# Gate columns turned, one modulation unit per slot, and no barrier before the context's projection

## The reference

```
a = rms_norm(h, norm_mix_pre)
z = a @ w_in                                  # 2048 x 4656
u, g_lru, q, kc, vc, ksel, vsel, kw, vw, gts = split(z)
y_lru = rglru_mixer(u, g_lru, ...)            # conv of 4 taps, gates, scan over time, times gelu
y_nsa = nsa_mixer(q, kc, vc, ksel, vsel, kw, vw, gts, ...)
y = concat(rms_norm(y_lru), rms_norm(y_nsa))  # then @ w_out, post norm, residual
```

## Time and profile before

| | us |
|---|---|
| runs | 2850.11, 2856.14, 2848.38 (median 2850.11) |
| the profiled execution | 2852.62, its span 2850.8 |
| PE busy | 2786.9 (98%) |
| DVE busy | 1748.4 (61%) |
| ACT busy | 1310.5 (46%) |
| POOL busy | 310.1 (11%) |
| chain that ended last, share on PE | 89% |

### The profile page before, as it was taken

How to read it: one execution, slowest core, us unless ns; L and a number is a source line. 1 busy time by engine, 2 the same in 40 slices (tenths; PEclk the granted TensorE clock), 3 DMA queues, 4 the chain that set the end, 5 groups by cost and what they waited for, 6 DMA issues and landing times.

```text
span 2850.8 us, 33136 instructions
## 1 busy us (share of the span) xinstructions
PE 2786.9 (98%) x13404; PEld 2188.3 (77%) x13404; DVE 1748.4 (61%) x2325; ACT 1310.5 (46%) x1912; POOL 310.1 (11%) x258
## 2 busy tenths in 40 slices
PE   8999899999989999999999999999999999999998
PEld 5777788888867777777777887887778888877786
DVE  4654646665646565565544664658876665788764
ACT  5362335554534344434533444454555454455553
POOL 0000100000022000001001110124201011321001
PEclk9999899999999999999999999999999999999999
DMA  8776474455588776767777756575345556454543
GB/s 300 272 264 239 162 261 162 155 207 199 185 276 287 251 244 218 254 222 251 255 261 244 263 200 206 190 253 168 126 142 179 204 191 201 164 170 132 171 172 123
DMA packets 293015, 600.34 MB, mean 211 GB/s; under 512 B 12514, under 2 KB 19370, under 8 KB 290944
## 3 DMA queue, kind: packets, MB, share of 16 engines
q1 hardware_dynamic: 279824, 548.07, 56.8%
q0 software_dynamic: 10656, 46.94, 4.4%
q10 hardware_dynamic: 2384, 3.22, 0.3%
HBM read 585.02 MB, written 13.17 MB: 210 GB/s over the span
## 4 chain that ended last, share of the span: by engine, by line
PE 89%; DVE 6%; DMA 2%; ACT 1%; POOL 0%; issue 0%; SPq 0%; DVEq 0%; ACTq 0%; POOLq 0%
PE ps L684 25%; PE ps L686 25%; PE ps L685 25%; PE ps L696 3%; DVE wlo L1838 2%; DVE bvx L2369 2%; PE ps L874 1%; PE ps L1106 1%; PE ps L1124 1%; PE ps L663 1%; PE ps L859 1%; DMA raw<-in_w_in_dram 1%; DMA raw<-in_mlp_w_dram 1%; ACT whi L1293 1%; PE ps L926 1%; PE ps L826 0%
## 5 line engine op out<-in xcount | busy, mean ns | idle before, releaser
L1838 DVE TENSOR_TENSOR wlo<-raw,whi 128x1024 fp32r<-128x1024 f32 x840 | 1040.6, 1263 | 774.6 <-ACT whi L1293 770.3
L1293 ACT ACTIVATE whi<-raw 128x1024 fp32r<-128x1024 f32 x840 | 868.8, 1050 | 1215.7 <-PE ps L686 809.0
L684 PE MATMUL ps<-whi,ay_hi 128*128 128x512 f32 x1728 | 689.4, 399 | 4.7 <-DVE ay_lo L2335 2.4
L686 PE MATMUL ps<-whi,ay_lo 128*128 128x512 f32 x1728 | 674.7, 390 | 0.0
L685 PE MATMUL ps<-wlo,ay_hi 128*128 128x512 f32 x1728 | 674.3, 390 | 0.0
L684 PE MATMUL ps<-whi,ax_hi 128*128 128x512 f32 (+1 forms) x1632 | 653.6, 400 | 9.9 <-DVE wlo L1838 7.5
L686 PE MATMUL ps<-whi,ax_lo 128*128 128x512 f32 (+1 forms) x1632 | 637.1, 390 | 0.0
L685 PE MATMUL ps<-wlo,ax_hi 128*128 128x512 f32 (+1 forms) x1632 | 636.7, 390 | 0.0
L684 PEld LDWEIGHTS ps<-whi,ax_hi 128*128 128x128 f32 x1632 | 310.8, 190 | 115.8 <-issue 41.6
L684 PEld LDWEIGHTS ps<-whi,ay_hi 128*128 128x128 f32 x1728 | 325.5, 188 | 83.1 <-issue 12.1
L686 PEld LDWEIGHTS ps<-whi,ay_lo 128*128 128x128 f32 x1728 | 325.1, 188 | 69.3
(11 more groups left out here) (478 smaller groups left out, 1996.9 us busy)
## 6 DMA issues: line engine op xcount, KB each, us to landing
raw<-in_w_in_dram SPq DMA_DIRECT2D x208, 1024.0 KB, 5.1
raw<-in_mlp_w_dram SPq DMA_DIRECT2D x128, 1024.0 KB, 6.4
raw<-in_w_mod_dram SPq DMA_DIRECT2D x96, 1024.0 KB, 7.4
raw<-in_w_out_dram SPq DMA_DIRECT2D x64, 1024.0 KB, 5.1
raw<-in_ple_gate_dram SPq DMA_DIRECT2D x16, 1024.0 KB, 5.1
z2c<-zsc POOLq DMA_DIRECT2D x13, 512.0 KB, 3.1
G<-bias_d ACTq DMA_DIRECT2D x4, 768.0 KB, 6.3
h<-in_ctx_dram POOLq DMA_DIRECT2D x1, 2048.0 KB, 8.5
```

The costliest lines, as they stand in the source:

```text
L684: mm(dst, hi_[:, kk, tt], whi[:, x.s % 2, k, 0:w], start=(nth == 0), stop=False)
L686: ins = mm(dst, lo_[:, kk, tt], whi[:, x.s % 2, k, 0:w], start=False, stop=(nth == KT - 1))
L1293: A(whi[:, x.s % 2, 2 * kh:2 * kh + 2, 0:w], raw[:, x.slot, 2 * kh:2 * kh + 2, 0:w], ACT.Copy).then_inc(hi_ready, 1)
L1838: V.tensor_tensor(wlo[:, x.s % 2, ks, 0:w], raw[:, x.slot, ks, 0:w], f32v(whi[:, x.s % 2, ks, 0:w]), ALU.subtract).then_inc(lo_ready, 1)
```

## The change

- `MOD0_AT` puts one modulation unit behind each unit from 3 to 34: chunk m in slots 3+4m to 6+4m. The column sums move into the middle of the unit after a chunk's last slot.
- `in1g` is one unit: its 16 row tiles by 48 columns are loaded in one transfer, the 48 columns become the stationary operand and 256 rows of the activations move: 48 products into 48 partitions. DVE copies the result (`zgT`, in the place of `modp_a`), PE transposes it back beside the first context unit, DVE scales it.
- The LRU's last steps lie one or two slots earlier, `prep("m2_01")` stands in slots 34 to 36, with `tmp` in `qT`'s place. The barrier is gone; waits on single semaphores stand for it. The high and low parts of the LRU's result are made in `nsa()`, slots 1 and 2.
- The start: the rest of x is issued when its first quarter has landed, the further weights when the first ones have.
- POOL copies h to memory first, then loads `cu`, `ca`, `cb` and the weights together; the sigmoid's product comes after the first squares.

```
-MOD0_AT = [(3, 4, 5, 6), (8, 9, 10, 11), (13, 14, 15, 16), (18, 19, 20, 20), (22, 23, 24, 25), (27, 28, 29, 29),
-           (31, 32, 33, 34), (36, 37, 38, 38)]
+MOD0_AT = [tuple(range(3 + 4 * m, 7 + 4 * m)) for m in range(8)]
...
-        for n in range(40):
+        for n in range(37):
...
                 if n == 1:
+                    sp.wait_ge(ev("x_in0"), 48)
                     sp.dma_start(h[:, :, CH:2 * CH], x_rows[:, :, CH:2 * CH]).then_inc(ev("x_in1"), 16)
                     sp.dma_start(h[:, :, 2 * CH:D], x_rows[:, :, 2 * CH:D]).then_inc(ev("x_in2"), 16)
+                    sp.wait_ge(raw_in[0], 16)
...
+                    if i == 2 and middle is not None:
+                        middle()
...
+            def gates_unit(x, A):
+
+                pe.wait_ge(lo_ready, 2 * x.s + 2)
+                pe.wait_ge(half_out, x.a - 1)
+                hi_, lo_ = A
+                w = GATES
+                dst = ps[0:w, half(x, 0)[1], 0:SEQ]
+                wh, wl = used(whi[:, x.s % 2], x), used(wlo[:, x.s % 2], x)
+                for k in range(KT):
+                    c_ = slice(k * w, k * w + w)
+                    one = mm(dst, wh[:, c_], hi_[:, k, :], start=(k == 0), stop=False)
+                    mm(dst, wh[:, c_], lo_[:, k, :], start=False, stop=False)
+                    ins = mm(dst, wl[:, c_], hi_[:, k, :], start=False, stop=(k == KT - 1))
+                one.then_inc(half_done, 1)
+                ins.then_inc(unit_used, 2)
...
+                def total():
+
+                    pe.wait_ge(ev("modp_in"), done[0] + 1)
+                    mod_columns(modp_a, 3)
+
+                if x.ph.name == "in1g":
+                    gates_unit(x, AX_)
+                else:
+                    hand_unit(x, AX_, total if done else None)
                 early(n)
                 for m_, at in enumerate(MOD0_AT):
-                    if n == at[3] + 1:
-                        pe.wait_ge(ev("modp_in"), m_ + 1)
-                        mod_columns(modp_a, 3)
...
-            boundary(pe, 0)
-
-
-            pe.wait_ge(half_out, 20)
-            pe.wait_ge(ev("modc_set"), MODSS)
-            prep("m2_01")
...
                 yield 0
+                pe.wait_ge(half_out, 20)
+                pe.wait_ge(ev("modc_set"), MODSS)
                 pe.wait_ge(a_lo, PR["m2_01"]["t0"] + 8)
+                for b in range(TB):
+                    ins = nc.tensor.transpose(ps[:, 7, b * GATES:b * GATES + GATES], zgT[:, b * P:b * P + P], eye[0:GATES, 0:GATES])
+                ins.then_inc(ev("nsa_gr"), 1)
...
-                yield 33
+                yield 31
                 dve.wait_ge(ev("lru_rms"), 1)
                 dve.wait_ge(ev("lru_y"), 2)
                 link(V.reciprocal(rsb[:, :], rsb[:, :]))
...
+                for first in (0, 2, 4):
+                    yield 34 + first // 2
+                    for g in range(first, first + 2 if first < 4 else 8):
+                        dve.wait_ge(ev("modc_set"), 5 + g // 2)
+                        prep("m2_01", [g])
...
-            for hf, hs in enumerate(halves):
-                dve.wait_ge(ev("lru_hi"), hf + 1)
-                V.tensor_tensor(ax_lo[:, hs, :], thT[:, hs, :], f32v(ax_hi[:, hs, :]), ALU.subtract)
-            boundary(dve, 2)
-
-
-            prep("m2_01")
+            dve.wait_ge(unit_used, 2 * IN1[-1].s + 2)
+            V.tensor_copy(zgT, ps[0:GATES, half(IN1[-1], 0)[1], 0:SEQ]).then_inc(half_out, TB)
...
-            for dst, src in ((ca[:, :, :], z2v[:, :, 5120:5632]), (cb[:, :, :], z2v[:, :, 5632:6144]),
-                             (cwpl[:, :, :], I["w_pool_2"][0].rearrange("g c d -> c g d")),
-                             (csub[:, :], bass.AP(I["subln_g_2"].tensor, I["subln_g_2"].offset, [[1, P], [1, 1]]))):
-                dma(dst, src).then_inc(ev("e_in"), 16)
             dma(h_d, h[:, :, :].rearrange("p b n -> p (b n)")).then_inc(ev("h_out"), 16)
...
             pool.wait_ge(ev("h_out"), 16)
-            dma(cu[:, :, :], z2v[:, :, 4096:4608]).then_inc(ev("e_in"), 16)
+            for dst, src in ((cu[:, :, :], z2v[:, :, 4096:4608]), (ca[:, :, :], z2v[:, :, 5120:5632]),
+                             (cb[:, :, :], z2v[:, :, 5632:6144]),
...
-            sigmoid_product()
```

More of the change, by code:

```diff
@@ L462, in chunk, with used, part @@
             return xs[UPC * i:UPC * i + UPC]
+        def used(t, x):
+            if x.ph.width == CH:
+                return t[:, :, :]
+            return t[:, :, :].rearrange("p a b -> p (a b)")[:, 0:KT * x.ph.width]
+        def part(t, x, kh):
+            w = used(t, x)
+            if x.ph.width == CH:
+                return w[:, 2 * kh:2 * kh + 2, :]
+            n_ = KT * x.ph.width // 2
+            return w[:, n_ * kh:n_ * kh + n_]
         def half(x, b):
@@ L617, in _ @@
                                  src[:, 8 * (x.u % 2):8 * (x.u % 2) + 8, :]).then_inc(raw_in[x.slot], 16)
+                elif x.ph.name == "in1g":
+                    sp.dma_start(used(raw[:, x.slot], x).rearrange("p (k n) -> p k n", n=GATES), x.ph.w[:, :, wcols(x.ph, 0)])\
+                      .then_inc(raw_in[x.slot], 16)
                 elif x.ph.kind == "pp":
@@ L666, in prep, with hand_unit @@
                     ins.then_inc(t_psum, 1)
-            def hand_unit(x, A):
+            def hand_unit(x, A, middle=None):
                 hi_, lo_ = A
-                w = x.ph.width
                 by_rows = x.u in (0, UPC - 1)
@@ L764, in lru @@
                 ins.then_inc(ev("lru_ss"), 1)
+                yield 34
+                pe.wait_ge(ev("lru_rms"), 1)
+                prep("m2_01", range(0, 2))
+                yield 35
+                prep("m2_01", range(2, 4))
+                yield 36
+                prep("m2_01", range(4, 8))
             early, beside = Beside(vectors()), Beside(lru())
@@ L798, in nsa @@
                 ins.then_inc(ev("nsa_qT"), 1)
-                for b in range(TB):
-                    ins = mm(ps[:, 7, b * GATES:b * GATES + GATES], flip[:, :], zgt[:, b, :], start=True, stop=True)
-                ins.then_inc(ev("nsa_gr"), 1)
                 for half_ in range(2):
@@ L804, in nsa @@
                     if half_ == 0:
+                        pe.wait_ge(ev("zgt_in"), 1)
+                        for b in range(TB):
+                            ins = mm(ps[:, 7, b * GATES:b * GATES + GATES], flip[:, :], zgt[:, b, :], start=True, stop=True)
+                        ins.then_inc(ev("nsa_gr"), 1)
                         pe.wait_ge(ev("nsa_qc"), 1)
@@ L1292, in hand_split @@
                         act.wait_ge(unit_used, 2 * (x.s - 2) + kh + 1)
-                    A(whi[:, x.s % 2, 2 * kh:2 * kh + 2, 0:w], raw[:, x.slot, 2 * kh:2 * kh + 2, 0:w], ACT.Copy).then_inc(hi_ready, 1)
+                    A(part(whi[:, x.s % 2], x, kh), part(raw[:, x.slot], x, kh), ACT.Copy).then_inc(hi_ready, 1)
             def root(n):
@@ L1421, in nsa @@
                 yield 1
-                act.wait_ge(ev("nsa_gr"), 1)
+                act.wait_ge(unit_used, 2 * IN1[-1].s + 2)
+                for hs in halves:
+                    A(ax_hi[:, hs, :], thT[:, hs, :], ACT.Copy).then_inc(ev("lru_hi"), 1)
+                yield 3
+                act.wait_ge(ev("nsa_gr"), 2)
                 A(gsig[:, :, :], ps[:, 7, 0:TB * GATES].rearrange("p (b n) -> p b n", b=TB), ACT.Sigmoid).then_inc(ev("nsa_gs"), 1)
@@ L2019, in nsa @@
                     yield 1 + half_
+                    if half_ == 1:
+                        for i, hs in enumerate(halves):
+                            dve.wait_ge(ev("lru_hi"), i + 1)
+                            ins = V.tensor_tensor(ax_lo[:, hs, :], thT[:, hs, :], f32v(ax_hi[:, hs, :]), ALU.subtract)
+                        link(ins)
                     dve.wait_ge(ev("nsa_kT"), half_ + 1)
@@ L2517, in _ @@
                     dma(t_[64 * e:64 * e + 64, :, 64 * e:64 * e + 64], v[e]).then_inc(ev("lru_w"), 16)
-            boundary(pool, 3)
+            pool.wait_ge(ev("lru_gates"), 4)
             for dst, src in ((w2k[:, :, 0, :], "cmp_w2_k"), (w2k[:, :, 1, :], "cmp_w2_k"), (w2v[:, :, :], "cmp_w2_v")):
```

92 lines of the change are left out of this document (49 added, 43 removed).

## The result

| kernel | median us | runs | profiled span | ratio to before |
|---|---|---|---|---|
| before | 2849.99 | 4 (2848.38 to 2856.14) | 2850.8 | |
| after | 2902.41 | 4 (2901.39 to 2905.33) | 2900.3 | 1.0186, 95% [1.0171, 1.0201] |

The change costs 52.4 us. The forecast was 2888 in a range of 2864 to 2908: the direction held and so did the main mechanism, the size was 14 us short.

What follows compares the result with a forecast made beforehand. TensorE, busy 98% of the span, was taken as the bound. The terms 56 + 8 - 19 - 2 - 5 = +38 us, added to the median 2850.1, gave 2888 us, with an 8-in-10 range of 2864 to 2908.

Steps and rivals of the forecast that it cites:

- A: Modulation in consecutive slots: seven new PE waits for modc plus longer waits for column sums; +56 us, bounds 40 and 65.
- The 52.0: Sum in us of seven delays from unit's end to mod_set, slots 7 to 31, taken as PE's waits for modc.
- the 10.0: Delay in us from unit's end to mod_set in slot 23, forecast as the longest of the seven waits.
- The 4 for the sums: Us added for PE waiting on ScalarE's copy of the totals, with column sums now in the middle of units.
- B: PE at half clock behind the new waits: six falls, less 1.6 us already paid; +8 us, between 0 and 16.
- C: Gates as one turned unit without barrier, from unit 35's end through the first context unit; -19 us, between -12 and -26.
- D: Staged first loads at the start let the first weights land earlier; -2 us.
- E: Pooling loads moved: PE's 3.3 us wait for Pool's squares goes, low-part waits shrink 1.7; -5 us, between 0 and -8.
- Loads become the bound: Rival, first stage: weight loads at 298 GB/s stretch each slot to 7.04 us, 32 slots +12; 2900 us; chance 0.12.
- Barrier changes its name: Rival, first context unit: the wait for half_out 19 grows until C gives nothing; 2907 us; chance 0.05.
- The removal wins: Rival: mod_set reaches PE in time, A and B about 0, seven waits together under 26 us; 2824 us; chance 0.07.
- Short waits: Rival: splits ready earlier, each chunk boundary costs about 4 us (28 in all), few clock falls; 2854 us; chance 0.06.

Runs made afterwards that it cites:

- run 2: Kernel after, with ScalarE's copy of the modulation's totals moved first in each slot; 2892.67 us, ratio 1.0149 to before.
- run 1: Kernel after, with VectorE's writing of the modulated columns (mod_set) moved first in each slot; 2851.75 us, ratio 1.0004 to before.
- second pair of traces: Kernels before and after run once more, unchanged, for a second trace of each; 2850.67 us (ratio 1.0001) and 2906.88 us (ratio 1.0195).
- Run 9: Kernel before with consecutive modulation units and both copies first, its old gates, barrier, first loads and pooling loads kept; 2852.61 us, ratio 1.0006.
- run 6: Kernel after with the first loads no longer staged, all issued at once; 2904.44 us, ratio 1.0185 to before.
- run 3: Kernel after with both edits, totals first on ScalarE and modulated columns first on VectorE; 2834.18 us, ratio 0.9942 to before.

## Why the prediction was right, and where its size was off

- **A, waits of the modulation: the path right; the sum right by luck.** +56 was forecast; the two kinds are 60.9 now and 1.7 before, so +59.2. But it was 52.0 + 4 and is 41.0 less 0.5, and 19.9 less 1.2: two errors of 11 and 15 us that cancel. The 52.0 took delays from a stretch where PE never stopped. In slot 23 the 10.0 held 3.8 us in which DVE waited for a split of weights that had not landed; after, that split was ready (DMA share 0.65 against 0.79 over the stage), and the wait is 6.0. Slots 7, 15 and 31 held 1.3, 2.6 and 1.7 us of the same kind; after, only 0.6 in slot 15 is left. These four make 8.8 of the 11 us. That the loads catch up because PE stops is argued from this; the stops in the middle of units are at most a part, since run 2 takes 13.6 us of them away and gets only 1.9 back on modc, most of it in slot 11 (6.5 to 8.0). So the longest wait is in slot 27 (7.4) and not near slot 23. In slot 11 DVE came late to the copy from taps; after, it stood idle before it, and the wait is 6.5 and not 8.3. The 4 for the sums was a guess from one slot, and there too low: in slot 7 ScalarE's copy comes 7.3 us after the middle of the unit, not 3.9: the split ahead of it starts only at 65.78, when its weights land, and then come two squares of 1.9 and a table load. Runs 1 and 2 show both terms singly.
- **B, clock: mis-sized.** +8 was forecast. The loss up to unit 35 is +17.6, and 1.6 more follows the 2.2 us wait. Six falls of 1.6 were counted. There are ten: all seven waits for modc are followed by a low clock, and so are the stops of 7.3, 1.6 and 6.8 us in the middle of units 7, 11 and 23 (not those of 0.9, 2.1 and 1.2). Each costs 1.9 on the mean, since modulation products and column sums run at half speed too (1.94 against 1.06, 1.87 against 1.05). This is the term that was furthest off in the sum.
- **C, gates and barrier: the path right, its worth too high.** For the stretch 17.6 was forecast and 17.5 measured; its wait in the first context unit was put at 4.3 (from +10.2 to +14.5) and is 3.1, the wait for the bank 2.4 and is 2.2. But 8.4 us of work moved ahead of the mark, not 5.8, because the first two turned groups (1.09 us) and a second column sum are among it, and the wait for the bank brings 1.6 of clock. In the traces C is 27.3 less 8.4, 2.2 and 1.6 = 15, against 19. And of the 44.9 us that it replaces, 10.5 were clock loss in the first trace of before (0.66 granted from 275 to 315); in the second trace that stretch lost 4.6 (0.79), and in the second pair of traces the stretch goes from 40.8 to 20.1 us, 20.7 less and not 27.3. Run 9 puts C, D and E at 16, against 26.
- **D, staged loads: nothing**, where -2 was taken (run 6).
- **E, pooling loads: right in its first part.** -5 was forecast, -3.4 is in the first pair of traces (+60.9 to +57.5) and -4.3 in the second. The wait for Pool (3.3) is gone. Of the 1.7 taken for the low parts hardly anything came: PE's waits for them in the MLP are 5.2 before and 4.9 after, only the longest shrinks (4.8 to 3.4).
- **No term for the last stage.** There 2.4 us are gained, for the wait that Pool's addition causes.
- **Rivals.** "Loads become the bound" would give nearly the right time, 2900, but it fails as the bound: PE waits 0.2 us for low parts in the first stage, the DMA share is 0.65, and run 1 gets the time back with the same loads. What there is of it are the 5 to 6 us of stops for the totals that runs 2 and 3 leave. "Barrier changes its name" falls by the 17.5. "The removal wins" and "Short waits" fall by the rows: the seven waits are 41.0 us together, not under 26 or 28. A range judged by its time alone would not have told these apart.

Added up against the first pair of traces, everything as after less before: waits and other idle 58.5, clock 19.2, and C without the 1.6 of clock behind its wait, -27.3 + 8.4 + 2.2 = -16.7, give +61.0 at the block matrix (60.9 read; D is inside); E and what follows up to the last stage -2.4; the last stage -9.0 (some -6.6 of clock, which is chance, and -2.4 of the wait); end +49.5.

**What stays open.** Why the same wait drops the clock in one execution and not in the next isn't settled. In run 3 the two reorderings give 7.8 us more together than singly. In the traces most of it is clock: up to the block matrix the loss is 20.4 after, 14.4 and 22.2 in runs 1 and 2, and 8.2 in run 3, so 8.0 more than the two single differences, and idle time 1.6 more. Why is not shown, and single traces of one kernel differ by as much. What part of the change takes the wait for `ay_lo` away isn't known either.

## What to carry to other kernels

When units of a side job are moved closer together, look at the consumer's place in each engine's slot, not at its length: operations of 0.2 to 0.6 us in the last place of a slot cost 41 us of waits, and moving them to the first place brought that back, and some clock with it. Do this before tightening the schedule; then the free slot can be kept as well, and it was still worth 10 us. A delay read from a stretch in which the bound engine never stopped can contain waits for others (weights here) that are not there in the changed kernel, and one trace's clock loss may be chance: a second trace of the unchanged kernel prices that for one run.

## What the hardware did unexpectedly

- Two executions of the same kernel differ by 7.7 us of span, with the waits of PE the same within 2.3 us each; clock loss is 19.3 us in one (12.1, 1.6 and 5.6 up to the turned q, up to the last stage and in it; windows of 5 us) and 9.7 in the other. The runs of before spread from 2842 to 2858.
- In the kernel after the clock is low behind all nine waits of 3.2 to 7.4 us in the first stage, behind one of the four of 0.9 to 2.1 (that of 1.6), and in the kernel before also behind the 1.2 us one of the earlier trace rows. Behind the 3.1 us wait in the first context unit it stays at 1.00 in the first trace of after and is low in the second. But the 3.3 us wait at the MLP of before was followed by 1.00 in one trace (820 to 840 us) and, at 3.5 us, by 0.83 in the other.
- Products with 48 stationary and 256 moving columns run at 0.119 us, against 0.111 for 48 moving columns and 0.227 for 512: half the columns of the last, half its time. The 48 moving columns, beside 128 stationary ones, gain hardly more.
- One of DVE's low parts (128x512) takes 5.08 us and not 0.69 while Pool adds two 128x2048 operands, and PE waits 2.4 us for what follows.
